# The fourth block of modulation weights goes to a buffer of its own, and one group of identity transposes leaves

## The reference

```
mod = silu(c) @ w_ada + b_ada            # 1024 x 6144 -> shift, scale, gate for both sub-layers
h   = rms_norm(x) * (1 + scale_mix) + shift_mix
z   = h @ w_in                           # 1024 x 7168: sc_x | sc_B | sc_C | u | v | gate_A | gate_B
yA  = sc_B * causal_dwconv3(sc_C * sc_x)
yB  = gelu(u) * (tril(W_s) @ layer_norm(gelu(v)) + b_s)
x   = x + gate_mix * ((sigmoid(gate_A) * yA + sigmoid(gate_B) * yB) @ w_out)
h   = rms_norm(x) * (1 + scale_ffn) + shift_ffn
x   = x + gate_ffn * moe(h)              # top 4 of 32 experts, clamped SwiGLU, 3 x 1024 x 1024 weights each
out = rms_norm(x)
```

## Time and profile before

| | |
|---|---|
| device time, median of 3 runs | 1239.52 us (1238.1 to 1242.1) |
| span of the profiled execution, first to last instruction | 1238.4 us |
| TensorE matmuls busy | 980.0 us (79%) |
| VectorE, ScalarE busy | 449.5 us (36%), 351.2 us (28%) |
| DMA, read from HBM | 466.00 MB, 377 GB/s over the span |
| first V product starts | 38.40 us |

### The profile page before, as it was taken

One profiled execution on the slowest core, in us unless ns is written; L12 is line 12 of the kernel. 1 busy time (PEld: TensorE's weight loads), 2 busy tenths in 40 slices (PEclk: granted clock), 3 DMA queues, 4 the chain that ended last, 5 costly groups with the idle time before them and its releaser, 6 DMA issues.

```text
span 1238.4 us, 23246 instructions
## 1 busy us (share of the span) xinstructions
PE 980.0 (79%) x9327; PEld 492.0 (40%) x9328; DVE 449.5 (36%) x1085; ACT 351.2 (28%) x735; POOL 8.4 (1%) x20
## 2 busy tenths in 40 slices
PE   6999999978787898976859967678788676657565
PEld 3788989743233233332213322223333222212122
DVE  0656555543344244442314432323343322322212
ACT  1544424422233133331213331212332212211113
POOL 0200000000000000000000000000000000000000
PEclk9999999989999899998889989989899888988778
DMA  9979587879999989999998789999969999999994
GB/s 360 373 274 348 183 321 253 332 291 425 423 425 424 422 361 426 424 423 422 424 428 352 313 338 426 423 425 423 406 266 422 424 425 424 424 423 424 423 424 197
DMA packets 60443, 468.93 MB, mean 379 GB/s; under 512 B 5148, under 2 KB 6468, under 8 KB 24484
## 3 DMA queue, kind: packets, MB, share of 16 engines
q1 hardware_dynamic: 60324, 467.06, 91.7%
HBM read 466.00 MB, written 1.05 MB: 377 GB/s over the span
## 4 chain that ended last, share of the span: by engine, by line
PE 55%; DMA 26%; issue 12%; DVE 5%; ACT 1%; SPq 1%; DVEq 0%; ACTq 0%
PE B L1205 30%; DMA W<-in_w_down_dram 26%; PE B L953 15%; PE B L1214 4%; PE B L973 2%; PE B L1157 2%; DVE EW L880 1%; DVE EW L877 1%; DVE EW L883 1%; ACT EW L573 1%; DMA raw<-in_w_ada_dram 1%; PE B L980 1%; PE B L1262 0%; PE B L1030 0%; SPq L359 0%
## 5 line engine op out<-in xcount | busy, mean ns | idle before, releaser
L1205 PE MATMUL B<-W,mT 128*32 128x256 f32 (+1 forms) x5888 | 548.5, 519 | 89.8 <-DMA W<-in_w_gate_up_dram 37.1
L1205 PEld LDWEIGHTS B<-W,mT 128*32 128x32 f32 x5888 | 194.9, 115 | 427.7 <-issue 271.6
L584 ACT ACTIVATE hT<-hT 32x256 bf16<-32x256 bf16 x368 | 152.6, 415 | 235.4 <-DVE hT L897 227.5
L877 DVE TENSOR_SCALAR EW<-B 128x256 f32<-128x256 f32 x46 | 19.5, 425 | 420.4 <-PE B L1205 420.4
L1214 PE MATMUL B<-b_gu,mT 128*32 128x512 f32 x368 | 61.8, 731 | 138.2 <-issue 138.2
L573 ACT ACTIVATE EW<-EW 128x256 f32<-128x256 f32 x46 | 19.2, 416 | 434.6 <-DVE EW L877 434.6
L953 PE MATMUL B<-hh,wh 128*128 128x256 f32 x384 | 109.9, 286 | 0.0
L953 PE MATMUL B<-hl,wh 128*128 128x256 f32 x384 | 108.6, 283 | 0.0
L953 PE MATMUL B<-hh,wl 128*128 128x256 f32 x384 | 108.6, 283 | 0.0
L667 DVE TENSOR_TENSOR wl<-raw,wh 128x2048 fp32r<-128x2048 f32 x32 | 72.8, 2313 | 72.7 <-ACT wh L466 72.7
L466 ACT ACTIVATE wh<-raw 128x2048 fp32r<-128x2048 f32 x32 | 59.6, 1907 | 111.5 <-DMA raw<-in_w_in_dram 76.8
(11 more groups left out here) (205 smaller groups left out, 711.1 us busy)
## 6 DMA issues: line engine op xcount, KB each, us to landing
W<-in_w_gate_up_dram SPq DMA_DIRECT2D x128, 2048.0 KB, 30.1
W<-in_w_down_dram SPq DMA_DIRECT2D x63, 2048.0 KB, 23.2
raw<-in_w_in_dram SPq DMA_DIRECT2D x13, 2048.0 KB, 8.4
raw<-in_w_ada_dram SPq DMA_DIRECT2D x12, 2048.0 KB, 12.2
raw<-in_w_out_dram SPq DMA_DIRECT2D x2, 2048.0 KB, 10.2
raw<-in_w_in_dram SPq DMA_DIRECT2D x2, 1024.0 KB, 11.4
W<-in_w_down_dram SPq DMA_DIRECT2D x2, 1024.0 KB, 37.8
x_sb<-in_x_dram SPq DMA_DIRECT2D x1, 1024.0 KB, 4.8
```

Source lines behind the costliest of these rows:

```text
L584: A(ys[CAP * m:CAP * m + CAP, g * QC:(g + 1) * QC], yp[CAP * g:CAP * g + CAP, m, :], ACT.Copy).then_inc(y_moved, 1)
L877: V.tensor_scalar(halves(gs), paired(GU[:, 0:QC]), LIMIT, None, ALU.min).then_inc(gmin_ready, 1)
L1205: t = M(o, src[:, k % KQ, CAP * (k // KQ):CAP * (k // KQ) + CAP], w, start=(first and k == 0), stop=(k == KT - 1))
```

## The change

Unit 3, the fourth modulation block, no longer goes through the ring: it is issued at once, behind units 0 to 2, into slot 5 of `W` (the memory of `wh1`), with a semaphore of its own, `s_aside`. Every later unit takes the ring buffer one place earlier (`place(n)`), so that units 4, 5 and 6 wait for the product of block 0, 1 and 2 (before: unit 3, 4, 5 and 6 for blocks 0, 1, 2 and 3). From unit 7 on each unit waits for the same predecessor as before. ScalarE waits for four modulation products before it writes `wh1`. The 24 identity transposes between the products of blocks 0 and 1 are left out; those before blocks 2 and 3 stay. `PLACE` is renamed to fit the shifted ring.

```diff
-        PLACE = (1, 2, 8, 0, 3, 4, 5, 6, 7, 9)
+        PLACE = (0, 1, 8, 2, 3, 4, 5, 6, 7, 9)
...
+        ASIDE = 3
+
+        def place(n):
+            return n if n < ASIDE else n - 1
+
         def raw_slot(n):
-            return raw[:, (n % RING) * UW:(n % RING + 1) * UW]
+            if n == ASIDE:
+                return slot(5)
+            return raw[:, (place(n) % RING) * UW:(place(n) % RING + 1) * UW]
+
+        def landed(n):
+            if n == ASIDE:
+                return s_aside, 16
+            return s_slot[place(n) % RING], 16 * (place(n) // RING + 1)
...
-                if n >= RING:
-                    m = n - RING
+                if n != ASIDE and place(n) >= RING:
+                    m = n - RING if n - RING > ASIDE else n - RING - 1
                     if m in ada_units:
                         sp.wait_ge(ada_used, ada_units.index(m) + 1)
...
-                    sp.dma_start(dst, src).then_inc(s_slot[n % RING], 16)
+                    sp.dma_start(dst, src).then_inc(landed(n)[0], 16)
...
             split_high(0, (1,))
+            act.wait_ge(ada_used, 4)
             split_high(1)
...
             for q in range(1, 4):
-                keep_warm(WARM_LOAD, B[5])
+                if q > 1:
+                    keep_warm(WARM_LOAD, B[5])
                 modulation(0, q)
```

More of the change, by code:

```diff
@@ L211, in hybrid_trunk @@
         ranks = B[4][:, 0:3 * E]
-        s_x = sem("s_x"); s_rows = sem("s_rows"); s_bada = sem("s_bada"); s_bada_rest = sem("s_bada_rest"); s_first = sem("s_first"); s_gffn = sem("s_gffn")
+        s_x = sem("s_x"); s_rows = sem("s_rows"); s_bada = sem("s_bada"); s_bada_rest = sem("s_bada_rest"); s_first = sem("s_first"); s_aside = sem("s_aside"); s_gffn = sem("s_gffn")
         s_ws = sem("s_ws"); s_bs = sem("s_bs"); s_lng = sem("s_lng"); s_rw = sem("s_rw")
@@ L328, in _ @@
                     sp.dma_start(dst[:, 0:k, :], src[:, 0:k, :]).then_inc(s_first, 16)
-                    sp.dma_start(dst[:, k:KT, :], src[:, k:KT, :]).then_inc(s_slot[n % RING], 16)
+                    sp.dma_start(dst[:, k:KT, :], src[:, k:KT, :]).then_inc(landed(n)[0], 16)
                 else:
-                    sp.dma_start(dst, src).then_inc(s_slot[n % RING], 16)
+                    sp.dma_start(dst, src).then_inc(landed(n)[0], 16)
                 if n == ada_units[3]:
@@ L359, in load @@
                     sp.dma_start(unit_slot(u).rearrange("p (g n) -> p g n", g=2), dn_v[e, j - NQ]).then_inc(s_unit[u % SLOTS], 16)
-            assert [n % RING for n in (NU - 3, NU - 2, NU - 1)] == [1, 2, 0]
+            assert [place(n) % RING for n in (NU - 3, NU - 2, NU - 1)] == [0, 1, 2]
             sp.wait_ge(split_l, SPLITS * (len(split_units) - 2))
@@ L462, in split_high @@
                     else:
-                        act.wait_ge(s_slot[n % RING], 16 * (n // RING + 1))
+                        act.wait_ge(*landed(n))
                     if j >= 2 and c == 0:
@@ L943, in arrived @@
             def arrived(n):
-                pe.wait_ge(s_slot[n % RING], 16 * (n // RING + 1))
+                pe.wait_ge(*landed(n))
             def split_ready(j, k):
```

## The result

The changed kernel takes 1232.99 us (median of 6 runs, 1231.0 to 1233.24), the kernel before 1239.38 us (6 runs, 1238.1 to 1242.1): ratio 0.9938, 95% interval 0.9927 to 0.9950. It is faster by 0.62%, 6.4 us, where I forecast 0.3 us and gave "faster by over 0.3%" a chance of 0.06.

What follows compares the result with a forecast made beforehand. The prediction took the compute chain up to the first V product, with transfers pacing the prologue, to bound the kernel. Its terms summed to -0.3 us, other parts and clock at 0: 1239.5 to 1239.2 us, range 1236.8 to 1241.8.

Steps and rivals of the forecast that it cites:

- the costing of the 24 transposes: TensorE between the first two products: 2.6 to 2.8 us gross gain, net 0.5 on this path, 0.3 in the sum.
- the renamed slots: Slots 0 to 3 and the ring shifted by one, experts' units included: same releases and buffer kinds, worth nothing.
- The prologue's sum: Chain up to the first V product: transfers pace it, start at 38.1 us in place of 38.40, -0.3 us.
- The currency: Start of the first V product: a microsecond won or lost there reaches the end about one for one.
- the clock's fall: TensorE at the V product's start: eight matmuls 0.42 us apart against 0.23 after idle, priced at 1.54 us.
- The clock: New idle before the fourth product: a fall there or before V counted 0 together; rival 1240.5 us, chance 0.27.
- The crowded queue: Rival at the weight transfers: V's second unit, issued sooner, delays V's first half by 5.4 us; 1244.6 us, chance 0.05.
- The full return of the transposes: Rival in the prologue: all 2.77 us of the removed transposes come back, 1236.8 us, chance 0.13.

Runs made afterwards that it cites:

- b_minus24: The kernel before with only the 24 identity transposes between the first two products left out, ring and slots as before: 1232.6 us, ratio 0.9933.
- a_pad48: The changed kernel plus 48 TensorE instructions that only raise an unread semaphore, ahead of the first product: 1239.99 us, ratio 0.9992.
- a_early24: The changed kernel with the 24 transposes put back ahead of the first product, in TensorE's idle time: 1240.5 us, ratio 1.0002.
- a_keep24: The changed kernel with the 24 transposes put back between the first two products: 1240.3 us, ratio 1.0000.
- a_dead126: The changed kernel plus 256 TensorE instructions ahead of the first product, 252 never executed and 4 for the branch: 1234.09 us, ratio 0.9944.
- b_pad208: The kernel before plus 208 TensorE instructions that only raise an unread semaphore: 1257.69 us, ratio 1.0141.
- a_nop48: The changed kernel plus 48 empty TensorE instructions, which the build dropped, so a repeat of the changed kernel: 1234.49 us, ratio 0.9943.
- b_rot: The kernel before with its three ring buffers only renamed and PLACE as in the changed kernel: 1240.33 us, ratio 0.9998.
- the five kernels with 133: Kernels with 3461 TensorE instructions ahead of the loop (rest by 256: 133): the kernel before, b_rot, a_keep24, a_pad48, a_early24; ratios 0.9992 to 1.0002.

## Why the prediction was wrong

**The step that failed** is the costing of the 24 transposes. I priced what leaves by the time in which it ran, 2.6 to 2.8 us gross and 0.3 net, and gave the experts' stage no term of its own; the one sentence on it, on the renamed slots, says "Nothing; no instruction changes". An instruction has a place in the program as well as a duration, and 48 of them ahead of a loop of jumps change where that loop stands in the blocks that TensorE fetches. In place of 0, this term measured: experts 4.6 us shorter (933.85 to 929.25), found again with the same prologue as before (b_minus24), absent with the changed prologue and the old length (a_pad48, a_early24, a_keep24), and present again when instructions that never run move the loop by 256 (a_dead126, against the three with the old length). The Trainium skill has the rule, "Runtime: NRT & Kernel Launch", Instruction fetch mechanics: the sequencer refills instructions in blocks of 256, and a taken branch out of the fetched window stalls for the fetch. I had not weighed it. Both runs at 256 more agree with that period: experts 928.1 and 928.9 us against 929.25, and the stop again 27 matmuls in. The net 4.6 us are 6.5 us less at the pause of the queue and 1.9 us more elsewhere. Two views could have warned me. The chain by engine has 12% of "issue", which I passed over (9% after the change). And TensorE's waits over the experts have 20.9 us of "issue" inside runs of equal matmuls, for which the profile names no engine and no transfer.

**The prologue's sum held in its mechanism.** V product 0.6 us earlier for a forecast 0.3: the fourth block's wait ended at 28.25 (28.7), V's first half at 31.74 (32.2), both 0.4 us sooner, the rest as worked out. At the old program length the block set aside gives ratios of 0.9992 to 1.0002 (a_pad48, a_keep24, a_early24): at most 0.1%, as forecast. An early issue into a full queue bought nothing.

**The currency held.** A late start of the first round by 21.9 us with the experts 4.95 us shorter made 17.0 at the end (b_pad208). Of the 7.1 us between the two profiled spans, 2.5 lie ahead of the first round. The V product starts 0.6 us sooner and is spared the clock's fall. Part of that was given back at the wait for a later unit (ScalarE's split of it starts at 62.15 us before and at 62.18 after), and at the mixer's end 1.5 us are left: VectorE's work there starts at 244.85 us in place of 246.35. The other 1.0 us lies at the entry to the loop, where the granted clock is 0.66 from 266 to 276 us before and 0.83 after. Most of the 2.5 belongs to the execution and not to the change: in a_nop48, the same program, the first round comes at 279.67 us, 0.75 sooner than before.

**The clock.** The new gap before the fourth product (1.61 us) brought no fall, and the gap before the V product brought one in one of two executions of one program. Across programs it is as open: 1.84 us of idle had a fall behind it in the kernel before and in b_rot, 1.85 us in a_keep24 had none. I was right to count it in neither direction, and wrong to take one execution's fall as a property of that gap.

**The rivals.** The crowded queue did not happen: V's first half came sooner, though the queue was held 5.15 and 6.03 us at the issues behind it. The full return of the transposes did not happen either, though its number was nearest to the result: 2.8 us were offered and 0.6 taken. No rival had the cause.

**What stays open.** The runs show that the position decides, that 256 more bring the same time back, which stops move, and at which place the time is won. That the stops are waits for blocks of the program is the rule above and fits the packets that start inside them (24 of 27 stops); the profile itself names no releaser for a stop. The runs do not show which jump costs what, nor why the five kernels with 133 stop twice at the pause, for 6.8 to 7.8 us in all, and every other one once, for 2.1 to 3.9 us. I know of no rule that would have given the size beforehand.

## What to carry to other kernels

An edit that adds or removes instructions ahead of a loop with branches has a second effect that has nothing to do with what it does; here it was 0.6%, twenty times the forecast effect of the edit. Before such a gain is credited to an idea, run the edit with its length put back (instructions in idle time, or in a branch never taken), and the old kernel with the new length. In the profile, look for idle time put down to "issue" inside a run of equal instructions, and count at which instruction of the run it stands in both kernels; compare the packets of kind "instruction"; and look for the stops where the stream of transfers stands still, since those reach the end.

## What the runs showed of the hardware that I had not expected

- A stop of 3.5 to 4.0 us in the middle of a run of equal matmuls, at a fixed place of the program; it moved by 24 matmuls when 24 matmuls and their weight loads left the program far ahead of it, and came back to its place at 256 instructions more.
- The number of instruction blocks fetched tells the slow group from the others: 109 against 103 to 105; the four longest stops have three such fetches inside before and two after, and are 2.0 to 2.9 us shorter.
- Stops of TensorE were worth their time only where the weight stream stood still: 5.7 us fewer there made that pause 6.5 us shorter, while some 13 us fewer over the rest of the experts gained nothing (892.27 us before, 894.18 after).
- 160 instructions that are never executed made the kernel 0.3% faster than the changed one (0.9913 against 0.9938); TensorE then enters the loop without a stop.
- Instructions on TensorE that only raise a semaphore are dear: 80 more of them delayed the first product from 22.93 us (with 128) to 35.25 us (with 208), 0.15 us each. With 48 it starts at 11.93 us, since they fit into time in which TensorE waits for the first block anyway.
- The sync queue was held for 5.15 and 6.03 us at issues that otherwise take 0.4, while the DMA engines stayed busy.
